# Recurrent mixer from norm to scan in one block: keys first, preparation tile by tile beside the projections

## The chip, the cores and the metric

One core of a Trainium2 chip. The metric is the device time of one execution in microseconds (us), the median of the runs. The engines are TensorE (PE in the profile, its weight loads PEld), VectorE (DVE), ScalarE (ACT), GpSimd (POOL) and SyncE (SP), which issues the weights' DMAs. Each has its own queue and runs it in order; they meet only at semaphores.

## What is computed

The whole kernel is a stack of four layers, each with a mixer and a feed-forward, on 512 tokens of width 1024. The change lies in the mixer of the second layer:

```
xx = token_shift(h) - h;  x_j = h + xx * mu[j]        # j: r, w, k, v, a, g
r, k, v = xr @ w_r, xk @ w_k, xv @ w_v
w = -softplus(-(w0 + tanh(xw @ w1) @ w2)) - 0.5
a = sigmoid(a0 + (xa @ a1) @ a2);  g = sigmoid(xg @ g1) @ g2
kk = k * k_k, each head (64 columns) divided by its length
k = k * (1 + (a - 1) * k_a);  decay = exp(-exp(w))
S_t = S_(t-1) diag(decay_t) - (S_(t-1) kk_t)(kk_t a_t)^T + v_t k_t^T;  y_t = S_t r_t
y = group_norm(y) * ln_w + ln_b + sum(r * k * r_k) * v
out = (y * g) @ w_o
```

The recurrence is computed in chunks of 128 tokens for 16 heads. A token's rates are summed within its chunk, and powers of the decay turn r, k, kk and kk*a into "hats", with which a chunk is matrix products and one triangular system. That system is solved by inverting diagonal blocks of 32 (a substitution of 31 steps) and three rounds of products.

## The kernel before

Activations lie transposed: 8 tiles of 128 features x 512 tokens (2 KB of a partition each) in `arena`, in groups of eight named XN, XX, MX, RR, KK, VV, WW, AA. A weight matrix streams through a ring of four slots in units of 128 x 1024. ScalarE copies each unit to a rounded type (`split_high`, L298, two buffers `high_r`), VectorE subtracts to get the rest (`split_low`, L303), and TensorE makes three products per block of 128 x 128 (`products`, L280 to L284), 24 per unit. The split of unit n+2 waits for unit n's products. `split_and_read` interleaves a unit's split with what ScalarE or VectorE do with finished tiles. The order of streams is `ORDER`; SyncE loads by it, always four units ahead.

`phase` opens a block: all engines meet at its end, and GpSimd clears its semaphores after it, one by one. The mixer (`rwkv`) is such blocks one after another:
- `rms_norm` (L472 to L484): sum of squares by TensorE, root on ScalarE, reciprocal and scaling on VectorE;
- the token shift (L771), and lora1 loaded;
- the low rank (L777 mixes on VectorE, L813 products): three inputs of 8 tiles in turn. GpSimd splits the mix for r (L786, L788);
- streams r, k, v. VectorE mixes ahead for the next one, GpSimd splits, ScalarE copies the results (L853);
- second low rank (L884) with sigmoids (L891), rates in WW and in-rates in AA;
- k * k_k, then `norm` per head (L443 to L484);
- k's factor, 32 scans (L922) that sum the rates, centring at token 64, subtraction, and GpSimd's r * k with ScalarE's r_k and TensorE's sums for the bonus (L943, L949, L956);
- three exponents of a whole group (L966 to L969) and four products of a whole group (L979 to L988);
- diagonal blocks: products (L1068), copies by ScalarE (L1089), v turned to tokens (L1076), transposes L1036 and L1039, and the substitution of the first half on VectorE (L1052, L1055);
- the scan: 16 units of four heads and one chunk; unit u is chunk u // 4, heads 4 * (u % 4) on, so a unit's state was last changed four units earlier. Masks L1305, states L1342 and L1344. The second half's substitution runs on GpSimd beside it;
- group norm (L1394 to L1406, square L1416, root L1418) with GpSimd's product of bonus and v (L1411), transposes, the gate.

## Time and profile before

| | |
|---|---|
| median of 3 runs | 3280.72 us (3279.76 to 3281.08) |
| the profiled execution: time, span | 3279.62 us, 3277.8 us |
| TensorE busy | 2874.6 us, 88% |
| VectorE, ScalarE, GpSimd busy | 1609.5, 997.7, 628.9 us |
| mean granted clock of TensorE | 0.928 |

A row of the timeline gives the start and length in us, the engine, the line and operation, what it writes and reads, how many were merged, and in brackets how long the engine stood idle before it and what ended that. A clock of 1.00 is 2.4 GHz, 0.50 is 1.2 GHz. An f32 product has two records, one of the rounded type has one.

### The profile page before, as it was taken

To read this page: it belongs to the slowest core of one execution; us is meant where nothing else is said; L and a number is where in the kernel's file an instruction comes from. 1 tells how busy PE (TensorE), PEld (TensorE's weight loads), DVE (VectorE), ACT (ScalarE), POOL (GpSimd) and SP (SyncE) were. 2 spreads that over 40 slices of the span, in tenths; PEclk is the share of its full clock that TensorE was granted. 3 is DMA by queue.
4 is the path that set the end of the run, shared out by engine and by line. 5 is a ranking of instruction groups with operands and counts; after the bars stand their busy time and mean duration, and the time that the engine had idled before them with its cause. 6 is when DMAs were issued, how large, how long until landed. Compare 5 with 4: busy or idle time off the path is not lost. (4 is left out here: it accounts for less than half of the span.)

```text
span 3277.8 us, 37985 instructions
## 1 busy us (share of the span) xinstructions
PE 2874.6 (88%) x13832; PEld 2279.5 (70%) x13832; DVE 1609.5 (49%) x2033; ACT 997.7 (30%) x1493; POOL 628.9 (19%) x573
## 2 busy tenths in 40 slices
PE   6799999698449959999979967579999987999999
PEld 4678888276248947888858856258888863688887
DVE  3377763621663457775342546555443335764432
ACT  3233332122231213333223243243222223732221
POOL 0031112320221003111100033253111101431110
PEclk9899999799678979999989977789999998999999
DMA  3123333122000002333313200113323320023333
GB/s 126 61 71 96 96 90 96 40 84 77 0 1 1 1 8 84 96 96 90 103 53 96 83 1 1 34 26 101 96 96 90 103 84 7 2 90 96 96 89 104
DMA packets 79432, 218.67 MB, mean 67 GB/s; under 512 B 21808, under 2 KB 21936, under 8 KB 78800
## 3 DMA queue, kind: packets, MB, share of 16 engines
q1 hardware_dynamic: 78880, 213.28, 21.5%
q10 hardware_dynamic: 432, 3.78, 0.3%
q8 instruction: 76, 1.25, 0.2%
q14 instruction: 44, 0.36, 0.0%
HBM read 214.93 MB, written 2.10 MB: 66 GB/s over the span
## 5 line engine op out<-in xcount | busy, mean ns | idle before, releaser
L280 PE MATMUL psum<-rounded,high_r 128*128 128x512 f32 x3104 | 1220.4, 393 | 61.1 <-DVE rounded L245 41.6
L282 PE MATMUL psum<-rounded,high_r 128*128 128x512 f32 x3104 | 1213.9, 391 | 0.0
L284 PE MATMUL psum<-rounded,ring_low 128*128 128x512 f32 x3104 | 1213.3, 391 | 0.0
L303 DVE TENSOR_TENSOR ring_low<-ring,high_r 128x1024 fp32r<-128x1024 f32 (+2 forms) x432 | 519.2, 1202 | 734.0 <-ACT high_r L298 732.7
L298 ACT ACTIVATE high_r<-ring 128x1024 fp32r<-128x1024 f32 (+2 forms) x432 | 421.2, 976 | 1490.8 <-PE psum L284 1466.8
L280 PEld LDWEIGHTS psum<-rounded,high_r 128*128 128x128 f32 x3104 | 586.4, 189 | 200.0 <-issue 51.2
L284 PEld LDWEIGHTS psum<-rounded,ring_low 128*128 128x128 f32 x3104 | 586.5, 189 | 122.8
L282 PEld LDWEIGHTS psum<-rounded,high_r 128*128 128x128 f32 x3104 | 587.0, 189 | 121.2 <-issue 1.0
L655 DVE TENSOR_TENSOR arena<-psum,inverse 128x512 f32<-128x512 f32 x176 | 121.5, 691 | 313.7 <-PE psum L284 313.5
L555 POOL CAST rounded<-rows 128x512 f32 (+1 forms) x88 | 53.8, 612 | 785.3 <-DVE rows L660 785.3
L1598 POOL TENSOR_SCALAR arena<-arena,small 128x512 f32<-128x512 f32 x64 | 99.6, 1563 | 196.8 <-DVE small L1567 195.8
L396 POOL TENSOR_TENSOR arena<-resid 128x512 f32<-128x512 f32 x49 | 63.9, 1303 | 335.5 <-DVE resid L384 335.5
L557 POOL TENSOR_TENSOR rounded<-rows,rounded 128x512 f32 (+1 forms) x88 | 115.8, 1316 | 13.2 <-POOL rounded L555 11.9
L455 PE MATMUL psum<-work,const 128*128 128x512 f32 x116 | 64.7, 721 | 54.0 <-ACT work L443 54.0
L401 POOL TENSOR_TENSOR square_sum<-square_sum,arena 128x512 f32<-128x512 f32 x49 | 90.8, 1853 | 3.8
L455 PEld LDWEIGHTS psum<-work,const 128*128 128x128 f32 x116 | 26.5, 236 | 90.8 <-ACT work L443 61.9
L384 DVE TENSOR_TENSOR resid<-psum,resid 128x512 f32<-128x512 f32 (+1 forms) x64 | 44.3, 692 | 88.2 <-PE psum L284 88.2
L516 PE MATMUL psum<-const,arena 128*128 128x128 f32 x216 | 34.2, 334 | 54.1 <-PEq L111 54.1
L1491 PEld LDWEIGHTS psum<-const,arena 128*128 128x128 f32 x384 | 43.5, 146 | 54.0 <-issue 50.3
L1993 POOL TENSOR_TENSOR arena<-arena,rows 128x256 f32<-128x256 f32 x32 | 21.5, 686 | 298.8 <-SPq L111 282.9
L624 ACT ACTIVATE work<-arena,vec 128x512 f32<-128x512 f32 x88 | 71.1, 808 | 12.5 <-DVE arena L655 12.5
L1479 PE MATMUL psum<-arena 64*128 64x512 f32 x192 | 61.4, 726 | 15.2 <-DVE arena L1546 11.3
(256 smaller groups left out, 2836.7 us busy)
## 6 DMA issues: line engine op xcount, KB each, us to landing
ring<-in_up SPq DMA_DIRECT2D x176, 512.0 KB, 3.5
ring<-in_down SPq DMA_DIRECT2D x64, 384.0 KB, 3.1
ring<-in_down SPq DMA_DIRECT2D x64, 320.0 KB, 2.9
ring<-in_even_in SPq DMA_DIRECT2D x36, 512.0 KB, 3.5
ring<-in_sgu_in SPq DMA_DIRECT2D x16, 512.0 KB, 3.5
ring<-in_even_out SPq DMA_DIRECT2D x16, 384.0 KB, 3.1
ring<-in_qkv SPq DMA_DIRECT2D x12, 512.0 KB, 3.4
ring<-in_sgu_out SPq DMA_DIRECT2D x8, 512.0 KB, 3.5
```

The lines of the kernel that those rows point to most:

```text
L280: nc.tensor.matmul(psum[:, m, :], high_r[:, r % HIGHS, blk], x_high, start=(k0 + k == 0), stop=False)
L282: nc.tensor.matmul(psum[:, m, :], high_r[:, r % HIGHS, blk], x_low, start=False, stop=False)
L284: mm = nc.tensor.matmul(psum[:, m, :], ring_low[:, r % R, blk], x_high, start=False, stop=end)
L298: nc.scalar.activation(high_r[:, r % HIGHS, 0:nk * P], ring[:, r % R, 0:nk * P], ACT.Copy).then_inc(unit_high, 1)
L303: nc.vector.tensor_tensor(ring_low[:, r % R, 0:nk * P], ring[:, r % R, 0:nk * P], high_r[:, r % HIGHS, 0:nk * P].bitcast(F32), ALU.subtrac ...
L396: nc.gpsimd.tensor_tensor(square, x, x, ALU.mult).then_inc(squared, 1)
L401: nc.gpsimd.tensor_tensor(square_sum[:, :], square_sum[:, :], square, ALU.add).then_inc(squares_summed, 1)
L455: nc.tensor.matmul(psum[:, 4, :], gather(i), square_sum[:, :] if squares_ready else work[:, i % 4, :], start=(i == 0), stop=(i == sums - 1 ...
L557: nc.gpsimd.tensor_tensor(tile_of(rounded(HL, KF), n), rows[:, 2 + pair, :], tile_of(rounded(HH, KF), n).bitcast(F32), ALU.subtract).then_ ...
L624: nc.scalar.activation(work[:, r, :], zs(r), ACT.Identity, bias=v1(g * R + (cb + r)), scale=v1(g * R + (cw + 88 + r))).then_inc(biased, 1)
L655: nc.vector.tensor_tensor(zs(r), psum[:, r, :], inverse[:, 0, :], ALU.mult).then_inc(scaled, 1)
L1598: nc.gpsimd.tensor_scalar(x, x, one(rc, i, e), None, ALU.mult).then_inc(sem, 1)
```

## The change

All from the norm to the end of the scan becomes one block with 65 semaphores, and nothing in it meets but by these.
- The order of streams is k, r, v. The norm, shift (now GpSimd's), mix and split for k go tile by tile.
- While k is multiplied, VectorE mixes per unit one tile of the three low-rank inputs and of r's and v's; TensorE runs that tile's low-rank products after the unit. ScalarE squares the finished keys, and TensorE sums them.
- In stream r, TensorE runs rates (now by token, so with the bias w0 as a 65th row) and in-rates after units 0 to 3. After units 4 to 7 it spreads the inverse lengths and sums the rates by products with a centred triangular matrix (`spread_and_sum`), which takes the scans' place. ScalarE takes exponents of a tile (`raise_powers`), VectorE forms its hats.
- v is computed by token (`token_products`: activations stationary, weights moving), so it needs no transposes. Units 2 to 5 carry tiles 4 to 7 of the preparation, units 0, 1, 6 and 7 the diagonal blocks. Both substitutions are on GpSimd, the first beside the stream v.
- The scan's units go by groups of tiles: 8 units for the first 8 heads, two per chunk, then 8 for the others, so a unit's state was last changed two units earlier.
- The bonus is formed after the scan, from the hats (the powers cancel): 8 products on GpSimd, scaled by ScalarE, summed by TensorE.

The diff at its core:

```diff
-        ORDER = ["sgu_in", "sgu_out", "up0", "down0", "rwkv_r", "rwkv_k", "rwkv_v", "rwkv_o", "up1", "down1",
...
+        ORDER = ["sgu_in", "sgu_out", "up0", "down0", "rwkv_k", "rwkv_r", "rwkv_v", "rwkv_o", "up1", "down1",
...
+                    if after_unit:
+                        after_unit(g * st.body + r)
...
+            carried = [heads(XN + 7), heads(XX + 7)]
+            solved = [heads(XX + b) for b in range(2)]
...
+                c, i0 = u % 8 // 2, 4 * (u // 8) + 2 * (u % 2)
...
+            def changes(u):
+                return u % 8 < 6
...
+                    def gather(i):
+                        pe.wait_ge(squared, i + 1)
+                        nc.tensor.matmul(psum[:, 7, :], head_sums(i), inverse[:, i % 2, :], start=(i == 0),
+                                         stop=(i == KD - 1)).then_inc(gathered, 1)
+
+                    def low_rank(n):
+                        if n == 0:
+                            pe.wait_ge(lw1_loaded, 16)
+                            pe.wait_ge(guarded, 1)
+                        pe.wait_ge(low_rank_mixed, 3 * n + 3)
+                        for at, m, to, x in ((0, 64, psum[0:HD, 4, :], 0), (64, 64, psum[HD:P, 4, :], 1),
+                                             (128, 128, psum[:, 5, :], 2), (256, 32, psum[0:32, 6, :], 2)):
+                            mm = nc.tensor.matmul(to, lw1[:, n, at:at + m], low_rank_in[x], start=(n == 0), stop=(n == KD - 1))
+                        mm.then_inc(low_rank_used, 1)
+                        if n:
+                            gather(n - 1)
...
+                    def spread_and_sum(i):
+
+                        if i == 0:
+                            pe.wait_ge(kk_inverted, 1)
+                            pe.wait_ge(rates_kept, 8)
+                            pe.wait_ge(a_kept, 8)
+                        if i == 4:
+                            pe.wait_ge(diagonal_kept, 4 * BLOCKS)
+                        if i:
+                            pe.wait_ge(powered, i)
+                        if i >= 2:
+                            pe.wait_ge(hats_done, i - 1)
+                        nc.tensor.matmul(psum[:, 4 + i % 2, :], head_spread(i), inverse[:, 0, :], start=True, stop=True).then_inc(spread_done, 1)
+                        for c in range(NCH):
+                            for k in range(2):
+                                mm = nc.tensor.matmul(psum[:, 6 + k, c * CH:(c + 1) * CH], rates[:, c, i * P:(i + 1) * P],
+                                                      con("centred", P, k * P), start=True, stop=True)
+                        mm.then_inc(summed, 1)
+
...
+                        if n % 4 == 0:
+                            pe.wait_ge(hats_done, n + 4)
...
+                    def with_r(n):
+                        if n == 0:
+                            gather(KD - 1)
+                        if n < 4:
+                            for m in (2 * n, 2 * n + 1):
+                                rate(m)
+                                in_rate(m)
+                        else:
+                            spread_and_sum(n - 4)
+
+                    def with_v(n):
+                        if n in (0, 1):
+                            pair_of_units(2 * n)
+                            pair_of_units(2 * n + 1)
+                        elif n in (6, 7):
+                            pair_of_units(2 * n - 8)
+                            pair_of_units(2 * n - 7)
+                        else:
+                            spread_and_sum(n + 2)
+
...
+                    products(pe, "rwkv_k", two_parts(RR, VV), k_taken, lambda k: pe.wait_ge(k_low, k + 1), after_unit=low_rank)
+                    products(pe, "rwkv_r", two_parts(MX, WW), r_taken, lambda k: pe.wait_ge(r_low, k + 1),
+                             lambda m: pe.wait_ge(k_taken, 5 + m), after_unit=with_r)
+                    token_products("rwkv_v", two_parts(VV, XN))
...
+                    def after_k(g, m, done):
+                        n = 4 * g + m
+                        done()
+                        nc.scalar.activation(tile(KK + n), psum[:, m, :], ACT.Copy).then_inc(k_taken, 1)
+                        act.wait_ge(k_taken, n + 1)
+                        if n >= 2:
+                            act.wait_ge(gathered, n - 1)
+                        else:
+                            act.wait_ge(normed, KD)
+                        nc.scalar.activation(inverse[:, n % 2, :], tile(KK + n), ACT.Square, scale=col("k_k", n)).then_inc(squared, 1)
+                        if n == KD - 1:
+                            act.wait_ge(low_rank_used, KD)
+                            act.wait_ge(v_mixed, KD)
...
+                    def raise_powers(i):
+                        act.wait_ge(summed, i + 1)
+                        if i:
+                            act.wait_ge(hats_done, i)
+                        grow, shrink_before = powers(i)
+                        before = psum[:, 7, :].rearrange("p (c t) -> p c t", c=NCH)[:, :, 0:1].rearrange("p c o -> p (c o)")
+                        nc.scalar.activation(shrink_before, psum[:, 7, :], ACT.Exp, scale=-EXP_HALF)
+                        nc.scalar.activation(grow, psum[:, 6, :], ACT.Exp, scale=EXP_HALF)
+                        nc.scalar.activation(chunk_in[:, i, :], before, ACT.Exp, scale=EXP_HALF)
+                        nc.scalar.activation(shrink[:, :], psum[:, 6, :], ACT.Exp, scale=-EXP_HALF).then_inc(powered, 1)
+
...
+                    def k_rest(i):
+                        dve.wait_ge(k_high, i + 1)
+                        nc.vector.tensor_tensor(rounded(VV)[:, i, :], tile(VV + i), rounded(RR)[:, i, :].bitcast(F32),
+                                                ALU.subtract).then_inc(k_low, 1)
+
+                    def k_mix(i):
+                        dve.wait_ge(shifted, 2 * i + 2)
+                        mix(2, i, tile(VV + i)).then_inc(k_mixed, 1)
+                    for i in range(KD):
+                        nc.vector.scalar_tensor_tensor(out=tile(XN + i), in0=resid[:, i, :], scalar=col("mix_g", 8 + i), in1=inverse[:, 0, :],
+                                                       op0=ALU.mult, op1=ALU.mult).then_inc(normed, 1)
+                        if i >= 2:
+                            k_mix(i - 2)
+                        if i >= 3:
+                            k_rest(i - 3)
...
+                    def during_k(g, m, done):
+                        n = 4 * g + m
+                        if n == 0:
+                            dve.wait_ge(lw1_loaded, 16)
+                        else:
+                            dve.wait_ge(low_rank_used, n)
+                        for which, to in zip((1, 4, 5), low_rank_in):
+                            mix(which, n, to).then_inc(low_rank_mixed, 1)
+                        mix(0, n, tile(WW + n)).then_inc(r_mixed, 1)
+                        mix(3, n, tile(XN + n)).then_inc(v_mixed, 1)
+
+                    def hats(i):
+
+                        grow, shrink_before = powers(i)
+                        kk, k, a, r = inverse[:, 1, :], tile(KK + i), tile(AA + i), tile(RR + i)
+                        dve.wait_ge(spread_done, i + 1)
+                        nc.vector.scalar_tensor_tensor(out=kk, in0=k, scalar=col("k_k", i), in1=psum[:, 4 + i % 2, :],
+                                                       op0=ALU.mult, op1=ALU.mult).then_inc(hat_steps, 1)
+                        dve.wait_ge(hat_steps, 6 * i + 1)
+                        dve.wait_ge(powered, i + 1)
+                        nc.vector.scalar_tensor_tensor(out=whole_w(i), in0=kk, scalar=-1.0, in1=shrink_before,
+                                                       op0=ALU.mult, op1=ALU.mult).then_inc(hat_steps, 1)
+                        dve.wait_ge(hat_steps, 6 * i + 2)
+                        nc.vector.scalar_tensor_tensor(out=shrink_before, in0=a, scalar=-1.0, in1=k,
+                                                       op0=ALU.add, op1=ALU.mult).then_inc(hat_steps, 1)
+                        dve.wait_ge(hat_steps, 6 * i + 3)
+                        nc.vector.scalar_tensor_tensor(out=k, in0=shrink_before, scalar=col("k_a", i), in1=k,
+                                                       op0=ALU.mult, op1=ALU.add).then_inc(hat_steps, 1)
+                        nc.vector.tensor_tensor(a, a, kk, ALU.mult).then_inc(hat_steps, 1)
+                        nc.vector.tensor_tensor(r, r, shrink[:, :], ALU.mult).then_inc(hat_steps, 1)
+                        dve.wait_ge(hat_steps, 6 * i + 5)
+                        nc.vector.tensor_tensor(k, k, grow, ALU.mult)
+                        nc.vector.tensor_tensor(a, a, grow, ALU.mult)
+                        ends = shrink[:, :].rearrange("p (c t) -> p c t", c=NCH)[:, 0:3, CH - 1:CH].rearrange("p c o -> p (c o)")
+                        nc.vector.tensor_tensor(scl[:, i, 0:3], ends, chunk_in[:, i, 1:4], ALU.mult).then_inc(hats_done, 1)
+
+                    def during_r(g, m, done):
+                        n = 4 * g + m
+                        if n == 0:
+                            dve.wait_ge(gathered, KD)
+                            nc.vector.tensor_scalar(inverse[:, 0, :], psum[:, 7, :], 1.0, 1e-24, ALU.mult, ALU.max).then_inc(kk_guarded, 1)
+                            dve.wait_ge(kk_rooted, 1)
+                            nc.vector.reciprocal(inverse[:, 0, :], inverse[:, 1, :]).then_inc(kk_inverted, 1)
+                        if n >= 4:
+                            dve.wait_ge(r_taken, n - 3)
+                            hats(n - 4)
+
+                    def during_v(g, m, done):
+                        n = 4 * g + m
+                        if n == 1:
+                            dve.wait_ge(diagonal_kept, 4 * BLOCKS)
+                            turn_in(0).then_inc(turned_in, 1)
+                        if 2 <= n < 6:
+                            dve.wait_ge(r_taken, n + 3)
+                            hats(n + 2)
+                    split_and_read(dve, "rwkv_k", split_low, during_k)
+                    split_and_read(dve, "rwkv_r", split_low, during_r)
+                    split_and_read(dve, "rwkv_v", split_low, during_v)
+                    dve.wait_ge(diagonal_kept, 8 * BLOCKS)
+                    turn_in(1).then_inc(turned_in, 1)
+                    dve.wait_ge(steps0, SUBSTITUTED)
+                    turn_back(0).then_inc(turned_back, 1)
...
+                    part(MX, WW, r_mixed, r_high, r_low)
+                    pool.wait_ge(unit_done, r_first)
+                    part(VV, XN, v_mixed, v_high, v_low)
+                    pool.wait_ge(unit_done, v_first)
+                    identity(pool, 0, steps0)
+                    pool.wait_ge(turned_in, 1)
+                    substitute(pool, 0, steps0)
+                    pool.wait_ge(unit_done, v_end)
                     nc.gpsimd.memset(state, 0.0).then_inc(cleared, 1)
+                    pool.wait_ge(summed, KD)
                     for x in solved:
                         nc.gpsimd.memset(x, 0.0).then_inc(cleared, 1)
-                    identity(pool, steps)
-                    substitute(pool, nc.gpsimd, steps)
+                    pool.wait_ge(hats_done, KD)
+                    identity(pool, 1, steps1)
+                    pool.wait_ge(turned_in, 2)
+                    substitute(pool, 1, steps1)
...
+                    dve.wait_ge(bonus_done, 1)
+                    nc.vector.tensor_copy(bonus, psum[:, 0, 0:64]).then_inc(bonus_kept, 1)
...
+                    for i in range(KD):
+                        nc.gpsimd.tensor_tensor(arena[:, KK + i, :], arena[:, RR + i, :], arena[:, KK + i, :], ALU.mult).then_inc(paired, 1)
+                    pool.wait_ge(bonus_kept, 1)
+                    nc.gpsimd.tensor_tensor(vw, vw, bonus.unsqueeze(2).to_broadcast([P, 64, HD]), ALU.mult).then_inc(done, 1)
...
+                    for i in range(KD):
+                        act.wait_ge(paired, i + 1)
+                        nc.scalar.activation(arena[:, KK + i, :], arena[:, KK + i, :], ACT.Copy, scale=col("r_k", i)).then_inc(rated, 1)
```

## Rows read from the trace of the kernel before

**Rows 1.** Stretches: length, busy PE, PEld, DVE, ACT, POOL, TensorE's clock, DMA share, GB/s

```profile
587.00:654.00 67.00, 40.30 (x66) 8.60 (x66) 46.09 (x44) 6.73 (x8) 22.67 (x18) 0.72 0.05 18
...
803.00:850.00 47.00, 33.70 (x64) 13.41 (x64) 12.83 (x19) 17.66 (x26) 0.00 (x0) 0.86 0.05 10
...
850.00:920.00 70.00, 14.08 (x66) 14.03 (x68) 57.87 (x59) 17.93 (x13) 21.27 (x9) 0.53 0.00 0
...
920.00:958.00 38.00, 14.71 (x160) 13.14 (x159) 26.90 (x65) 15.95 (x40) 1.11 (x2) 0.68 0.00 1
...
958.00:1171.00 213.00, 200.14 (x1776) 190.58 (x1776) 85.60 (x185) 42.68 (x108) 35.26 (x67) 0.92 0.01 1
```

**Rows 2.** Timeline of VectorE, norm ahead of the mixer (start, length, operation)

```profile
591.73 3.35 DVE L475 RECIPROCAL rows<-rows 128x512 f32<-128x512 f32 x1 [0.70 <-ACT rows L445]
...
595.12 5.39 DVE L484 SCALAR_TENSOR_TENSOR arena<-resid,vec,rows 128x512 f32<-128x512 f32 x8
```

**Rows 3.** Timeline of ScalarE and VectorE at the end of one projection unit

```profile
783.76 1.06 ACT L298 ACTIVATE high_r<-ring 128x1024 fp32r<-128x1024 f32 x1 [3.90 <-PE psum L284]
...
784.86 1.23 DVE L303 TENSOR_TENSOR ring_low<-ring,high_r 128x1024 fp32r<-128x1024 f32 x1 [4.21 <-ACT high_r L298]
```

**Rows 4.** Timeline of VectorE and GpSimd, mixing and splitting

```profile
606.49 32.16 DVE L777 SCALAR_TENSOR_TENSOR arena<-arena,vec 128x512 f32<-128x512 f32 x32 [1.16 <-DVE arena L772]
...
663.85 1.29 POOL L788 TENSOR_TENSOR rounded<-arena,rounded 128x512 fp32r<-128x512 f32 x1
```

**Rows 5.** Timeline: TensorE in the low rank, ScalarE at the second one

```profile
627.41 25.46 PE L813 MATMUL psum<-arena 128*64 128x512 f32 x48 [0.72 <-DVE arena L777]
...
811.12 0.69 ACT L891 ACTIVATE arena<-psum,vec 128x512 f32<-128x512 f32 x1 [0.17 <-PE psum L884]
```

**Rows 6.** TensorE's granted clock around a gap (third column), and the gap's end

```profile
751.00:752.00 1.00, 0.00 (x0) 0.60 0.69 274
...
757.00:758.00 1.00, 1.00 (x4) 0.50 0.00 0
...
758.00:759.00 1.00, 1.00 (x5) 0.99 0.00 0
...
754.60 0.77 PE L280 MATMUL psum<-rounded,high_r 128*128 128x512 f32 x1 [5.73 <-PEq L111]
```

**Rows 7.** Timeline of TensorE, f32 products of 128 columns

```profile
926.30 1.97 PE L1076 MATMUL psum<-const,arena 128*128 128x128 f32 x16
...
931.45 2.06 PE L1068 MATMUL psum<-arena 64*128 64x128 f32 x32
```

**Rows 8.** The substitution's additions on both engines (min/median/max, first and last start)

```profile
L1055 POOL TENSOR_TENSOR rows<-rows,square_sum x31: 252/584/732, 961.9 to 998.4; 128x31 f32<-128x31 f32 x2, 128x60 f32<-128x60 f32 x2, 128x87 f32<-128x87 f32 x2, 128x112 f32<-128x112 f32 x2
```

**Rows 9.** Timeline of ScalarE and VectorE, diagonal blocks to the scan's first mask

```profile
932.65 6.38 ACT L1089 ACTIVATE arena<-psum 32x256 f32<-32x256 f32 x16
...
954.13 1.91 DVE L1039 STREAM_TRANSPOSE arena<-rows 128x1024 f32<-128x1024 f32 x1
...
960.43 1.29 DVE L1305 TENSOR_TENSOR arena<-psum,const 128x512 f32<-128x512 f32 x2 [2.62 <-POOL arena L1373]
```

**Rows 10.** Timeline of VectorE in the scan: state kept, next values kept

```profile
1127.33 0.29 DVE L1344 TENSOR_TENSOR spare<-spare,small 64x128 f32<-64x128 f32 x1
...
1134.50 0.42 DVE L1312 COPY work<-psum 128x256 f32<-128x256 f32 x1 [1.66 <-PE psum L1164]
```

**Rows 11.** Timeline of VectorE, ScalarE and GpSimd after the scan

```profile
1171.30 4.42 DVE L1394 TENSOR_REDUCE small<-arena 128x64 f32<-128x4096 f32 x1 [5.31 <-PEq L111]
...
1172.77 7.05 POOL L1411 TENSOR_TENSOR arena<-arena,small 128x4096 f32<-128x4096 f32 x1 [174.08 <-issue]
...
1175.75 4.12 DVE L1396 TENSOR_SCALAR small<-small 128x64 f32<-128x64 f32 x1
...
1184.37 3.62 ACT L1416 ACTIVATE arena<-arena 128x4096 f32<-128x4096 f32 x1 [13.37 <-DVE arena L1398]
...
1193.58 4.43 DVE L1406 TENSOR_TENSOR arena<-arena,small 128x4096 f32<-128x4096 f32 x1
```

More of the change, by code:

```diff
@@ L1013, in rwkv, with squares_of_blocks @@
[L1013 removed]
+            carried = [heads(XN + 7), heads(XX + 7)]
+            solved = [heads(XX + b) for b in range(2)]
+            def squares_of_blocks(x):
+                return x.rearrange("p (a b) -> p a b", b=BLOCK)
+            diagonal = [squares_of_blocks(flat(rows[:, 0:2, :])), squares_of_blocks(span(XX + 2, 2))]
+            lower = [squares_of_blocks(span(WW, 2)), squares_of_blocks(span(XX + 4, 2))]
+            inv_flat = [span(WW + 2, 2), flat(inverse[:, :, :])]
```

566 lines of the change are left out of this document (248 added, 318 removed).

## Prediction

> **What bounds the kernel now.** I read four views, in this order. First the stretches of the recurrent mixer [rows 1]: from the end of the feed-forward before it (587) to the first mask of the scan (960) lie 373 us, in which TensorE's big products are only the three projections. One projection unit costs 1.23 + 4.21 = 5.44 us from one split to the next [rows 3], so 24 units are 131 us. The other 242 us belong to small stages run one after another: norm, shift and low rank (67), low-rank seconds and key norm (47), scans and exponents (70, TensorE busy 14 and at half clock), diagonal blocks and substitution on VectorE (38). Second, VectorE's timeline for the lengths of one operation [rows 2, 4]. Third, TensorE's granted clock around idle gaps [rows 6]. Fourth, the handoffs after the scan [rows 11]. Everything outside 587 to 1198 is not touched; the constants' load at the start grows a little, which I leave out of the sum as well under 1 us.
>
> **The change, placed in absolute time.** The cheapest way to sum so large a rewrite is to rebuild the new block's time line with the old durations and to see when its first mask would come, against 960.4 now [rows 9].
>
> *Start to first key unit.* The inverse root is ready at 595.1 as now [rows 2]. Then VectorE does 24 operations (scale, mix, remainder of each tile), 0.67 us each alone [rows 2], 16 us; GpSimd computes the shifts beside it. Where both ran on SBUF, 32 mixes took 32.16 us, 1.0 each, half as much again [rows 4]. Between 16 and 24 I take 21.5: last operand at 616.6, and the unit that waits for it ends at about 618. The two ends are 613 and 621.
>
> *Key stream.* After each of its 8 units TensorE's queue holds `low_rank(n)`, which waits for three mixes. VectorE issues these behind `split_low` of unit n+2, and that waits for ScalarE's split, which waits for unit n itself (buffers of two). So TensorE idles per unit: the handoffs and 1.06 + 1.23 us give 2.6 [rows 3], three mixes 2.0, together 4.6 us. Behind that wait stand the next unit and all of TensorE's queue. Then four f32 products of 512 columns and the sum of squares of the keys. Their price: 24 such products took 25.46 us, 1.06 each [rows 5], in a stretch whose clock was 0.72 in the mean [rows 1]; the second low rank's took 0.69 + 0.17 = 0.86 each [rows 5]. I take 1.0 at full clock: 5.0 us. The clock: a gap from 749 to 754.6 brought it to half, and it was full again only at 758, 3.4 us after work resumed [rows 6]; half speed for 3.4 us loses 1.7 us. Bounds for this loss are 0 and 1.7 per unit. I take 1.7, because the gap of 4.6 us is near the one in the rows and comes after every unit. A cycle is 5.44 + 4.6 + 5.0 + 1.7 = 16.7 us. The first has no squares to sum and ends its low rank at 628.3; seven more end at 745.2. The whole low rank so costs more than the 46 us it takes alone today (606.5 to 652.9 [rows 4, 5]); it is not hidden beside the projection, but put between its units.
>
> *Receptance stream.* Units 0 to 3 are followed by two rate and two in-rate products each, and one last square sum: 4 x 5.44 + 17 x 0.93 (between 0.86 and 1.0) = 37.6. ScalarE reads each unit's four while TensorE works on the next unit, so its table loads there are covered; uncovered they would cost TensorE the difference once, at unit 0. Now at 782.8. Units 4 to 7 are followed by a spread (0.95) and eight products of 128 columns, 16 records in 1.97 us or 0.25 each [rows 7]: 5.44 + 0.95 + 2.0 = 8.4 each, 33.6, now 816.4. The 32 scans of VectorE are gone, as are the whole-array exponents and products. VectorE's own loop here is powers on ScalarE (three exponents at 0.69, one tiny, handoffs: 2.5) and then seven SBUF operations, 5.2 us: 7.7, just under TensorE's 8.4, so it hides if nothing disturbs it.
>
> *Value stream to first mask.* Times from its start at 816.4. Unit 0 ends at 5.4; the diagonal products wait for the fourth tile (7.7) and cost 16 x 0.13 us [rows 7], 9.8; unit 1 and two more pairs, 17.3; ScalarE's 8 copies at 0.40 and VectorE's transpose of 1.9 [rows 9] let GpSimd start substitution 0 at 22. It takes 37.5 us there [rows 8], on top of four tiles of VectorE work. Undisturbed, VectorE finishes tile 7 at 58; with its operations lengthened by half [rows 4], 7.8 + 2.5 = 10.3 per tile, at 67. Two pairs, unit 7, two pairs: 68 to 77. Copies, two transposes of 1.9 and handoffs: 74 to 83. The substitution, 59.5 alone, is at 70 to 83 by the same disturbance, and the scan waits for it. I take 80 of 74 to 86: first mask at 896.4. That is 64.0 us earlier. What was removed, the VectorE substitution above all, is inside that number.
>
> The Trainium skill (SBUF — State Buffer, "SBUF: two separate sides") says that a GpSimd operation and a VectorE operation with two SBUF inputs lock each other out for the whole instruction. The mixes show only half of that, 1.0 in place of 0.67 us [rows 4], while the small operation at 1175.75 did stand until GpSimd's long one ended [rows 11]. By full exclusion each tile would take about 9 us plus 2.5, and the value stream would end near 86; by the mixes, near 80. The sum goes by the mixes.
>
> *Scan.* Same 16 units and same order on each engine; only the state is read two units later instead of four. The state was written by 1127.6 and the read of the next unit but one cannot come before the next unit's values at 1134.5 are past [rows 10], so there are over 5 us of slack. Zero, with 0 to +3.
>
> *After the scan.* Now: sum at 0 (1171.30), square on ScalarE at 13.1, last product at 22.3 to 26.7 [rows 11]. New: GpSimd's queue clears 65 semaphores in place of 21, which now delay it by 1.5 us [rows 11], so 4.5; then eight products of 1.29 to 1.6 us [rows 4], ending at 16.0. ScalarE's eight rate copies are queued ahead of its square, so the square waits for the last of them: 16.9 in place of 13.1. Second sum ends at 25.1, the bonus is kept at 25.4, and only then starts GpSimd's product of 7.05 us, which today runs in the shadow. VectorE's last product would meet it, as the small operation at 1175.75 met it and took 4.12 us, to GpSimd's very end [rows 11]: 32.6 + 4.4 = 37.0 in place of 26.7. Cost +10.3, between +4 (no meeting) and +13.
>
> **Sum.** -64.0 + 10.3 = -53.7 us. The profiled span of 3277.8 becomes 3224; that execution took 3279.6, 1.8 more than its span, and the median of the three runs is 3280.72, so 3280.72 - 53.7 = 3227.
>
> **Rivals.**
> *The loss of clock is small and the engines don't disturb each other.* For it: gaps of 4.6 us are shorter than the one in the rows, and the clock fell only some 3 us into it. Against: there it stood at half when work resumed. It gives -13.6 (8 x 1.7), -5 in the value stream, -4 after the scan and -4 at the start: down to 3200.
> *VectorE becomes the bound from the receptance stream on.* Its loop of 7.7 us is 0.7 below TensorE's, with GpSimd at work beside it for most of the time. If each of the seven operations takes a third more, both streams go by it (+6), substitution gates the scan (+6), the rest goes to its upper ends (+3 start, +3 scan, +3 tail) and waits in the key stream are 0.8 us longer (+6): 3254.
> *TensorE stays at half clock through the key stream; slower than before.* Place: each gap of 4.6 us. If the 3.4 us to recover never run out, each unit costs 5.44 more and its five small products 3.3 beyond the 1.7: 8.7 x 8 = +70, 3297. It decides from seven of eight units on (7 x 8.7 = 61 > 54). Against it: after 754.6 the clock recovered in 3.4 us of steady work [rows 6], and a cycle here has over 10 us of it.
> *The scan gives it back.* If each of the 12 changing units waited 2 us for its state, +24: 3251, still faster. [rows 10] speak against it.
> *The work isn't hidden.* Of the 242 us of small stages the sum saves only 64 less 10; that the change hides less than its shape suggests is already in the forecast.
>
> **How the numbers follow.** Forecast 3227: 0.55. Undisturbed 3200 to 3215: 0.18. VectorE bound 3240 to 3254: 0.15. Scan: 0.03. Half clock: 0.04. Something not seen that takes over 50 us: 0.05, of which half ends within 0.2% or slower. The range 3200 to 3254 holds the first four, some 0.85. A run can tell 0.2% (6.6 us) from no change: faster 0.92, same 0.02, slower 0.06.
>
> **What would show it.** Key units at a period of 16.7 us with TensorE idle 4.6 in each and a granted clock near 0.8; receptance units 4 to 7 at 8.4; first mask at about 896; the square of the group norm behind the rate copies, and VectorE's last product of that norm ending 37 us after its first sum. Wrong would be: key units below 14 us, first mask after 915 or before 880, or a scan longer than 213 us.

## The result, and the profile after

The kernel after takes 3236.06 us (median of 4 runs, 3235.97 to 3237.95) against 3280.24 us for the kernel before on the same chip (4 runs, 3279.03 to 3281.08): a ratio of 0.9867, with a 95% interval of 0.985 to 0.9884. It is faster by 44 us, or 1.3%; the interval leaves out no change. The forecast was 3227, within 3200 to 3254. The profiled spans are 3277.8 and 3236.1 us, a difference of 41.7.

The stretches of the changed block are the first view of the kernel after, with the columns of [rows 1]:

```profile
587.00:618.00 31.00, 12.89 (x25) 6.97 (x26) 26.20 (x26) 6.95 (x10) 17.02 (x18) 0.51 0.16 55
618.00:748.00 130.00, 94.28 (x250) 43.31 (x249) 36.31 (x48) 20.74 (x27) 22.63 (x21) 0.79 0.10 33
748.00:820.00 72.00, 72.00 (x299) 49.78 (x298) 30.39 (x38) 33.32 (x52) 12.76 (x14) 1.00 0.19 59
820.00:900.00 80.00, 66.90 (x424) 55.26 (x423) 50.72 (x54) 31.11 (x66) 49.37 (x71) 0.94 0.17 53
900.00:1117.00 217.00, 201.66 (x1744) 192.13 (x1744) 86.11 (x187) 42.48 (x108) 31.19 (x59) 0.89 0.01 1
1117.00:1156.00 39.00, 14.11 (x65) 13.97 (x66) 25.34 (x8) 10.82 (x11) 21.08 (x9) 0.50 0.05 17
```

They are the start, the streams of k, r and v, the scan and what follows it. Only the stream r (748 to 820) fills TensorE at full clock. The stream k leaves 36 us of 130 idle and runs at 0.79. The first mask of the scan comes at 900.30 instead of 960.43 [rows 9], so the block gains 60.1 us up to there. Behind it two stages are longer than before. These are VectorE's rows in the kernel after that answer to [rows 9] and [rows 11]:

```profile
900.30 2.44 DVE L1370 TENSOR_TENSOR arena<-psum,const 128x512 f32<-128x512 f32 x4
...
1116.67 4.42 DVE L1493 TENSOR_REDUCE small<-arena 128x64 f32<-128x4096 f32 x1 [5.31 <-PEq L112]
...
1145.15 10.40 DVE L1507 TENSOR_TENSOR arena<-arena,small 128x4096 f32<-128x4096 f32 x1
```

From the first mask to the first sum the scan takes 216.4 us; before, 960.43 to 1171.30, it took 210.9: +5.5. From that sum to the end of the last product it takes 38.9 us; before it took 26.7: +12.2. The account is -60.1 + 5.5 + 12.2 = -42.4 us, against the 41.7 of the spans; the other 0.7 lies outside these stretches.

### The profile page after: what moved, and what is told of

It reads as the page before. It is cut to its first block and busy times, and to the rows that moved or that the text cites. A ratio compares the mean times of both kernels' runs of the same rounds, so it can differ in the third digit from the quotient of the medians.

```text
span 3236.1 us, 38094 instructions
## 1 busy us (share of the span) xinstructions
PE 2901.8 (90%) x13928; PEld 2294.1 (71%) x13928; DVE 1573.0 (49%) x1974; ACT 1000.3 (31%) x1522; POOL 666.3 (21%) x634
## 5 line engine op out<-in xcount | busy, mean ns | idle before, releaser
L281 PE MATMUL psum<-rounded,high_r 128*128 128x512 f32 x3040 | 1200.2, 395 | 65.3 <-DVE rounded L246 41.0
L283 PE MATMUL psum<-rounded,high_r 128*128 128x512 f32 x3040 | 1189.8, 391 | 0.0
L285 PE MATMUL psum<-rounded,ring_low 128*128 128x512 f32 x3040 | 1189.3, 391 | 0.0
L281 PEld LDWEIGHTS psum<-rounded,high_r 128*128 128x128 f32 x3040 | 574.6, 189 | 210.2 <-issue 56.7
L283 PEld LDWEIGHTS psum<-rounded,high_r 128*128 128x128 f32 x3040 | 575.5, 189 | 119.6 <-issue 2.6
L285 PEld LDWEIGHTS psum<-rounded,ring_low 128*128 128x128 f32 x3040 | 574.9, 189 | 120.5
L560 POOL TENSOR_TENSOR rounded<-rows,rounded 128x512 f32 (+1 forms) x88 | 116.4, 1323 | 13.1 <-POOL rounded L558 11.9
L458 PE MATMUL psum<-work,const 128*128 128x512 f32 x100 | 56.6, 730 | 48.8 <-ACT work L446 48.8
L904 PE MATMUL psum<-arena 128*64 128x512 f32 (+2 forms) x64 | 46.1, 1085 | 35.7 <-DVE arena L856 35.7
L1586 PE MATMUL psum<-arena 64*128 64x512 f32 x192 | 61.5, 727 | 15.1 <-DVE arena L1653 11.2
```

The lines of the kernel that those rows point to most:

```text
L281: nc.tensor.matmul(psum[:, m, :], high_r[:, r % HIGHS, blk], x_high, start=(k0 + k == 0), stop=False)
L283: nc.tensor.matmul(psum[:, m, :], high_r[:, r % HIGHS, blk], x_low, start=False, stop=False)
L285: mm = nc.tensor.matmul(psum[:, m, :], ring_low[:, r % R, blk], x_high, start=False, stop=end)
L458: nc.tensor.matmul(psum[:, 4, :], gather(i), square_sum[:, :] if squares_ready else work[:, i % 4, :], start=(i == 0), stop=(i == sums - 1 ...
L560: nc.gpsimd.tensor_tensor(tile_of(rounded(HL, KF), n), rows[:, 2 + pair, :], tile_of(rounded(HH, KF), n).bitcast(F32), ALU.subtract).then_ ...
```

## The experiments

All edits are to the kernel after, unless said otherwise. Single runs have no interval. They are read by their profiles, and the change in their time only serves as a check.

**The wait in the stream k.** The first two experiments ask what a unit's period consists of. In the kernel after, one period looks like this on VectorE (splits and mixes) and TensorE (low-rank products):

```profile
635.10 1.22 DVE L306 TENSOR_TENSOR ring_low<-ring,high_r 128x1024 fp32r<-128x1024 f32 x1 [10.96 <-ACT high_r L301]
636.24 3.39 DVE L856 SCALAR_TENSOR_TENSOR arena<-arena,vec 128x512 f32<-128x512 f32 x5
...
652.16 1.23 DVE L306 TENSOR_TENSOR ring_low<-ring,high_r 128x1024 fp32r<-128x1024 f32 x1 [12.52 <-ACT high_r L301]
...
638.36 5.83 PE L904 MATMUL psum<-arena 128*64 128x512 f32 x8 [4.45 <-DVE arena L856]
644.12 1.36 PE L894 MATMUL psum<-inverse,const 128*128 128x512 f32 x2
```

The split at 635.10 had itself waited 10.96 us for ScalarE, the mixes stand behind it, and TensorE stands for them. The period is 652.16 - 635.10 = 17.06 us. The first experiment only puts VectorE's mixes ahead of its split:

```diff
-                    split_and_read(dve, "rwkv_k", split_low, during_k)
+                    split_and_read(dve, "rwkv_k", split_low, early=during_k)
```

> One edit to the changed kernel: VectorE issues the mixes of tile n ahead of the split of unit n+2 (from the second tile on), so they run while unit n is multiplied. Theory A (the changed kernel's key stream is long because TensorE waits for mixes queued behind a split, and because its clock falls in that wait): the 4.45 us of idle and the half clock both go; the period of a key unit falls from 17.06 to 5.44 + 4 x 1.05 + 0.9 = about 10.5 us, the granted clock in the stretch from 0.79 to 1.00, and seven such periods save 46 us: 3190 us. Rival B (the small products between the units, or VectorE, set the period, and the wait only takes a place that something else would take): the period stays above 14 us and the kernel above 3215 us.

Measured: 3189.26 us (3186.12 to 3191.64), ratio to the kernel before 0.9727 (0.971 to 0.9743). The first mask is at 848.03, 52.3 us earlier; scan and tail stay (215.9 and 38.9). These are VectorE and TensorE in two of its periods, and TensorE's weight loads in the second:

```profile
644.12 1.22 DVE L306 TENSOR_TENSOR ring_low<-ring,high_r 128x1024 fp32r<-128x1024 f32 x1 [4.28 <-ACT high_r L301]
646.01 3.40 DVE L856 SCALAR_TENSOR_TENSOR arena<-arena,vec 128x512 f32<-128x512 f32 x5 [0.67 <-PE psum L904]
653.70 1.22 DVE L306 TENSOR_TENSOR ring_low<-ring,high_r 128x1024 fp32r<-128x1024 f32 x1 [4.29 <-ACT high_r L301]
...
652.44 3.11 PE L904 MATMUL psum<-arena 128*64 128x512 f32 x8
655.48 1.13 PE L894 MATMUL psum<-inverse,const 128*128 128x512 f32 x2
...
652.44 0.20 PEld L904 LDWEIGHTS psum<-arena 128*64 128x64 f32 x4 [0.35 <-issue]
653.45 0.30 PEld L904 LDWEIGHTS psum<-arena 128*128 128x128 f32 x2 [0.81 <-issue]
654.51 0.14 PEld L904 LDWEIGHTS psum<-arena 128*32 128x32 f32 x2 [0.76 <-issue]
655.48 0.30 PEld L894 LDWEIGHTS psum<-inverse,const 128*128 128x128 f32 x2 [0.84 <-ACT inverse L1156]
```

The period is 653.70 - 644.12 = 9.58 us: 5.44 for the unit and 4.14 for the small products. That is theory A, with a period still shorter than its 10.5. From 629 to 701 TensorE is busy 72.00 of 72.00 us, at a clock of 1.00. The idle 4.45 us were the order of VectorE's queue and nothing else, since nothing else was changed. 7 periods x (17.06 - 9.58) = 52.4, which is the 52.3 at the mask. The medians differ by less, 3236.06 - 3189.26 = 46.8: the profiled execution, 3186.12, is the fastest of its four, two others took 3191, and why those are slower no profile shows. The rows also correct a price. Five f32 products of 512 columns take 4.1 us, not 5.0, because both 64-column products, which write different halves of the PSUM partitions, start within the one slot of 1.01 us between the loads at 652.44 and 653.45. The Trainium skill (TensorEngine Tiling (Array Packing), "Key Properties") says that separate tiles of the array can load and multiply in parallel; this trace agrees for two tiles of 64 columns.

The second experiment keeps the wait and fills it, so that only the clock changes:

```diff
+                        if n >= 3:
+                            pe.wait_ge(k_taken, n - 2)
+                        for _ in range(20):
+                            nc.tensor.matmul(psum[:, (n + 1) % 4, :], rounded(RR)[:, 0, 0:P], rounded(RR)[:, 0, :], start=True, stop=True)
                         pe.wait_ge(low_rank_mixed, 3 * n + 3)
```

The products stand ahead of that wait and nothing reads them; from n = 3 on they wait for `k_taken` n - 2, so that their bank is free.

> Order of the changed kernel kept; while TensorE waits for the mixes after each key unit it makes 20 products of the rounded type that nobody reads (20 x 0.227 = 4.5 us, as long as the wait). This leaves the wait and takes only the fall of the clock away. Theory A (the forecast took 1.7 us per unit for the clock): the period falls from 17.06 to about 15.4 us, the kernel by 12 to 13 us to about 3223 us. Rival B (the clock costs nothing there, the small products are just longer than 1 us): the period stays at 17.0 to 17.3 us and the kernel at 3236 to 3238 us.

Measured: 3214.73 us (one run), 21.3 below the kernel after; the stretches of e2 and of the kernel after:

```profile
618.00:724.00 106.00, 106.00 (x406) 68.30 (x405) 36.30 (x48) 19.70 (x26) 19.16 (x17) 1.00 0.12 40
```

```profile
638.00:644.00 6.00, 5.64 (x8) 0.98 (x8) 1.63 (x3) 0.00 (x0) 2.33 (x2) 0.50 0.00 0
644.00:646.00 2.00, 2.00 (x6) 1.26 (x6) 0.00 (x0) 0.00 (x0) 0.00 (x0) 0.84 0.00 0
646.00:651.00 5.00, 4.97 (x22) 3.75 (x20) 0.00 (x0) 0.00 (x0) 0.00 (x0) 1.00 0.00 0
```

With the wait filled, the period is 14.11 us (= 5.44 + 4.5 + 4.1) and the clock stays full. So the clock cost 17.06 - 14.11 = 2.95 us per unit. 7 x 2.95 = 20.7 is most of the 23.2 us by which the first mask comes earlier (877.15); the first period, 13.54 in place of 15.50, and the start give the rest. The second fence shows why it is not 1.7: after each wait the clock is at half from 638.4 to nearly 645, about 6.5 us, and [rows 6] had shown 3.4. The expectation of -12 to -13 missed this.

**The scan.** Between these kernels VectorE's copies of a unit's values (`z`, once a unit) serve as a ruler. At full clock most of their 15 intervals are 12.1 to 12.6 us; the first is 9.74, and a few lie between 10.8 and 13.8 at fixed places. Three are off in the kernel after: the first takes 15.09 us (9.74 before), and the sixth and seventh take 14.83 and 20.71. The kernel before has 13.73 and 20.56 at the seventh and eighth, and 14.95 at the third. The two copies that bound the first interval, then TensorE and its stretches at the start and in the middle of the scan, kernel after:

```profile
905.64 0.42 DVE L1377 COPY arena<-psum 128x256 f32<-128x256 f32 x1 [2.91 <-PE psum L1053]
920.73 0.42 DVE L1377 COPY arena<-psum 128x256 f32<-128x256 f32 x1 [1.26 <-PE psum L1053]
...
901.96 2.05 PE L1038 MATMUL psum<-arena 128*128 128x128 f32 x8 [5.83 <-ACT arena L1233]
...
982.37 0.59 PE L1051 MATMUL psum<-spare,work 128*128 128x128 f32 x2 [1.71 <-issue]
...
906.00:916.00 10.00, 9.88 (x58) 9.19 (x59) 2.17 (x6) 0.00 (x0) 8.90 (x15) 0.50 0.01 2
...
982.00:994.00 12.00, 11.63 (x60) 11.44 (x62) 2.21 (x7) 0.38 (x1) 0.00 (x0) 0.52 0.00 1
```

Ahead of the first carry TensorE stands 5.83 us, because the first substitution's result has to be turned by VectorE and spread by ScalarE while nothing else is left to multiply. That result was there long before, at 890.9. Its turn stands in VectorE's queue behind that of the second half's blocks, which waits for their last copies (14.18 us idle):

```profile
896.70 1.90 DVE L831 STREAM_TRANSPOSE arena<-arena 128x1024 f32<-128x1024 f32 x1 [14.18 <-ACT arena L1198]
898.52 1.90 DVE L834 STREAM_TRANSPOSE rows<-arena 128x1024 f32<-128x1024 f32 x1
```

No run exchanged the two. After the pause the clock is at half until 917. The fourth kernel fills that pause with products that nothing reads:

```diff
                     pe.wait_ge(diagonal_kept, 8 * BLOCKS)
+                    for _ in range(26):
+                        nc.tensor.matmul(psum[:, 7, :], rounded(VV)[:, 0, 0:P], rounded(VV)[:, 0, :], start=True, stop=True)
                     carry(0)
```

> Ahead of the scan's first carry, where TensorE stands idle 5.8 us for the first inverse, it makes 26 products that nobody reads. Theory A (the scan is 5.5 us longer than before because this pause leaves TensorE at half clock for the first 15 us): the clock stays at 1.00, the first unit takes about 10 to 12 us instead of 15.1, the kernel is 3 to 6 us shorter: 3230 to 3233 us. Rival B (the units by groups of tiles are longer by themselves): the scan stays at 216 us and the kernel at 3236 us.

Measured: 3223.26 us (one run), 12.8 below the kernel after, more than either theory gave. The mask is at 899.64 (900.30 in the kernel after), and the scan takes 203.6 us instead of 216.4. The scan of e4, to be read against the stretch from 900 to 1117 of the kernel after (clock 0.89):

```profile
899.00:1103.00 204.00, 191.22 (x1757) 181.61 (x1756) 86.06 (x186) 42.48 (x108) 31.41 (x59) 0.96 0.01 1
```

The first unit is at 9.74 again, 5.35 us less, and the stretch from the mask to the first copy falls from 5.34 to 4.05. Later profiles bear this out: the first interval is 9.73 and 9.74 in the two later kernels with the same filling, and 15.04 to 16.14 in the six changed kernels without it. So the half clock behind the pause costs 6.6 us, more than the whole +5.5. The scan of the kernel before was no scan at full clock either: by the intervals beside them its 14.95 holds 2.8 us of half clock and its 20.56 another 8.4. An estimate without them is 210.9 - 11.2 = 199.7 us, and the last kernel below, at full clock until 19 us before its end, takes 200.2. So the new order of units costs next to nothing, as forecast. The rest of the gain was not expected: the pair 14.83 and 20.71 has become 13.73 and 12.20 (9.6 us), and one later unit takes 15.32. Filling the start also moved or removed a half-clock stretch 80 us later; one run does not show which.

**The first substitution.** The fifth kernel cuts GpSimd's first substitution to one step of 31:

```diff
-                for n, t in enumerate(range(BLOCK - 1, 0, -1)):
+                for n, t in enumerate(range(BLOCK - 1, 0, -1) if b else [1]):
...
-                    dve.wait_ge(steps0, SUBSTITUTED)
+                    dve.wait_ge(steps0, 4)
```

> The first substitution, on GpSimd beside the value stream, is cut to one of its 31 steps (its result is then wrong; all other work is kept). Theory A (beside GpSimd's small operations VectorE's operations on SBUF take 1.0 to 1.2 us instead of 0.69, and with them its tile is the bound of the value stream): the last three tiles' period falls from 9.9 to about 8.1 us, the first mask comes some 6 to 8 us earlier (900.3 to 893), the kernel is 5 to 8 us shorter: 3228 to 3231 us. Rival B (TensorE's own work sets the end of the stream): the operations are shorter but the mask comes at 899 to 900 and the kernel stays at 3234 to 3236 us.

Measured: 3232.32 us (one run), 3.7 below the kernel after (its profiled span 5.6 below), where 5 to 8 were expected. VectorE's rows for one tile in the stream v, first the kernel after, then e5:

```profile
855.16 0.99 DVE L1318 SCALAR_TENSOR_TENSOR arena<-inverse,arena 128x512 f32<-128x512 f32 x1
856.19 0.99 DVE L1321 SCALAR_TENSOR_TENSOR arena<-arena 128x512 f32<-128x512 f32 x1
...
859.18 1.19 DVE L1327 TENSOR_TENSOR arena<-arena,shrink 128x512 f32<-128x512 f32 x1
```

```profile
860.78 0.69 DVE L1318 SCALAR_TENSOR_TENSOR arena<-inverse,arena 128x512 f32<-128x512 f32 x1 [1.36 <-ACT shrink L1191]
861.50 0.69 DVE L1321 SCALAR_TENSOR_TENSOR arena<-arena 128x512 f32<-128x512 f32 x1
...
864.11 0.68 DVE L1329 TENSOR_TENSOR arena<-arena 128x512 f32<-128x512 f32 x1
```

The substitution does lengthen VectorE's operations from 0.68 to between 1.0 and 1.2 us, and GpSimd pays as well: its substitution lasts from 840.8 to 890.9, 50.1 us against 37.5 alone [rows 8]. Without it the last tiles' period falls from some 9.9 us to 8.12, and the mask comes 11.0 us earlier, at 889.30, where 6 to 8 were expected. TensorE's row behind the last tile, first in the kernel after, then in e5, shows of what:

```profile
882.58 3.79 PE L960 MATMUL psum<-arena 64*128 64x128 f32 x32 [8.17 <-DVE small L1332]
```

```profile
873.64 2.06 PE L960 MATMUL psum<-arena 64*128 64x128 f32 x32 [1.06 <-DVE small L1332]
```

VectorE's last tile is ready 8.9 us sooner, and the half clock behind TensorE's wait of 8.17 us, 1.7 us on this row, goes with it. The end of the substitution itself did not hold up the mask: it is at 890.9, and VectorE turned the result only at 898.52. The pause ahead of the first carry is 5.82 us here too, though 30 of 31 steps are gone. But the scan then takes 222.2 us (+5.8), at a clock of 0.87, its first units 16.14 and 18.49 us. Half of what the earlier mask gave is lost to the clock. The mechanism of the stream v is confirmed: in its last tiles VectorE is the bound. The time does not follow from it alone.

**After the scan.** Two kernels take the tail apart. The third moves GpSimd's eight products r * k into the second half of the scan (tiles 4 to 7 into `work`, which is free by then):

```diff
+                    pool.wait_ge(steps1, SUBSTITUTED)
+                    pool.wait_ge(y_done, 8)
+                    for i in range(KD):
+                        nc.gpsimd.tensor_tensor(pair_at(i), tile(RR + i), tile(KK + i), ALU.mult).then_inc(paired_early, 1)
...
-                    for i in range(KD):
-                        nc.gpsimd.tensor_tensor(arena[:, KK + i, :], arena[:, RR + i, :], arena[:, KK + i, :], ALU.mult).then_inc(paired, 1)
```

> GpSimd's eight products of r and k for the bonus are moved from after the scan into its second half, where GpSimd has nothing to do. Theory A (after the scan ScalarE's square waits behind eight rate copies that wait for these products, and GpSimd's product of 7.05 us then meets VectorE's last one): the square starts 13 us after the first sum instead of 19, the bonus is kept early, the long product falls under VectorE's sums, and the stretch from the first sum to the end of the last product falls from 38.9 us to 27 to 29 us: 3225 us. Rival B (GpSimd beside the scan delays the state updates): the scan is 3 us or more longer and the kernel above 3229 us.

The seventh is the third without the long product of bonus and v:

```diff
-                    nc.gpsimd.tensor_tensor(vw, vw, bonus.unsqueeze(2).to_broadcast([P, 64, HD]), ALU.mult).then_inc(done, 1)
```

> As the kernel with the bonus products in the scan, and GpSimd's long product of v and bonus (7.05 us) left out, so the output lacks the bonus's weight. Theory A (VectorE's last product of the group norm takes 10.4 us because it stands until that product ends): it takes 4.4 us, the stretch from the first sum to its end 22.8 instead of 28.75 us, the kernel 6 us less than 3227.4: 3221 us. Rival B (the last product is slow by itself or by its operands): it stays at 10.4 us and the kernel at 3227 us.

Measured: 3227.38 us (3226.77 to 3228.38, ratio to the kernel before 0.9841, 0.9825 to 0.9857) and 3221.45 us (one run). The scan is unchanged (216.3), and the tail falls from 38.9 to 28.75 and to 22.8 us. GpSimd and ScalarE in the kernel after:

```profile
1121.26 14.03 POOL L1513 TENSOR_TENSOR arena<-arena 128x512 f32<-128x512 f32 x8 [185.53 <-SPq L112]
1144.22 7.05 POOL L1515 TENSOR_TENSOR arena<-arena,small 128x4096 f32<-128x4096 f32 x1 [8.92 <-DVE small L1501]
...
1135.96 3.60 ACT L1523 ACTIVATE arena<-arena 128x4096 f32<-128x4096 f32 x1
```

Its last product on VectorE in e3, with GpSimd's long one beside it, and then in e7:

```profile
1134.26 7.05 POOL L1520 TENSOR_TENSOR arena<-arena,small 128x4096 f32<-128x4096 f32 x1 [105.30 <-DVE small L1508]
...
1135.19 10.40 DVE L1514 TENSOR_TENSOR arena<-arena,small 128x4096 f32<-128x4096 f32 x1
```

```profile
1136.02 4.43 DVE L1514 TENSOR_TENSOR arena<-arena,small 128x4096 f32<-128x4096 f32 x1
```

In the kernel after, ScalarE's square comes 19.3 us after the first sum (13.1 before, [rows 11]), behind the eight products, and VectorE's last product stands until GpSimd's has ended at 1151.27. The first costs 6.2 us, the second 6.0 (10.40 against 4.43 alone): 12.2, the whole loss. Moving the eight products did more than end the first: the square now comes 9.1 us after the first sum, earlier than the 13.1 before, because GpSimd's long product no longer holds up the small operation between first sum and subtraction (4.12 us at 1175.75, [rows 11]). VectorE's subtraction, which had met the eight products, is also shorter (5.45 to 4.42). That is the gain of 10.1. It did not end the meeting with the long product, since the bonus is kept only behind VectorE's second sum. So the tail of 28.75 lies in the expected 27 to 29 by two errors that cancelled: the square 4 us earlier than expected, and the meeting, which was to go, still there. The seventh kernel shows the price of that meeting: without the long product the operation takes 4.43 us, as its theory A said.

**The three edits together**, e1, e3 and e4 in one kernel, and then that kernel with one more pause filled:

> The mixes ahead of the split, the bonus products in the scan and the filled start of the scan in one kernel. Alone they saved 46.8, 8.7 and 12.8 us against 3236.1. Theory A (they are three separate places on the path): the savings add up, 3236.1 - 68.3 = 3168 us. Rival B (the scan's clock depends on more than its start, so that its saving of 12.8 us is partly chance of this placement): 3172 to 3180 us.

Measured: 3170.17 us (3160.3 to 3171.64), ratio 0.966 (0.9642 to 0.9677). Mask at 849.25, tail 28.75. The time lies between the two forecasts. The scan takes 209.6 us and not e4's 203.6, as the rival had it, because the pair in the middle is there again, 14.66 and 20.86. The half clock begins where VectorE turns the second inverse and TensorE stands 1.70 us. The last kernel puts two f32 products, which nothing reads, into that stop:

```diff
+                        if u == 6:
+                            pe.wait_ge(y_kept, 5)
+                            for _ in range(2):
+                                nc.tensor.matmul(psum[:, 7, :], con("ident"), arena[:, VV, :], start=True, stop=True)
                         corrections_in(u)
```

> The kernel is e6_all_three with one thing added: ahead of unit 6's corrections, where TensorE stands 1.70 us while VectorE turns the second inverse (924.61 [1.70] in e6), it has two f32 products of 512 columns that nothing reads, about 1.0 us each. Theory A (the short stop itself sets off the half clock that lasts from about 926 to 945 in e6): the intervals between the z copies there, 14.66 and 20.86, become about 12.9 and 12.2, and the time falls by 9 to 10 us from 3170: 3160 to 3162; if the half clock then comes later in the scan, less. Rival B (the half clock comes at a place of its own, whatever this stop does): both intervals stay near 14.7 and 20.9, and the time is 3170 to 3171. Rival C (the products only delay the unit behind them): 3171 to 3172, with the interval of 14.66 longer by up to 0.5.

Measured: 3159.81 us (3158.69 to 3165.37), ratio 0.9639 (0.9623 to 0.9655), and the scan takes 200.2 us. The stretch of the stop, first in e6, then in e8:

```profile
924.00:930.00 6.00, 5.39 (x27) 5.42 (x28) 0.93 (x3) 0.03 (x1) 0.00 (x0) 0.58 0.00 0
930.00:936.00 6.00, 6.00 (x33) 5.78 (x34) 1.44 (x5) 0.38 (x1) 0.00 (x0) 0.50 0.00 0
936.00:942.00 6.00, 6.00 (x39) 5.43 (x37) 1.76 (x4) 0.00 (x0) 0.00 (x0) 0.50 0.00 0
942.00:948.00 6.00, 5.44 (x34) 5.33 (x34) 2.08 (x5) 1.83 (x5) 0.00 (x0) 0.71 0.01 3
```

```profile
924.00:930.00 6.00, 6.00 (x49) 5.29 (x48) 1.49 (x4) 0.53 (x2) 0.00 (x0) 1.00 0.00 0
930.00:936.00 6.00, 6.00 (x67) 5.57 (x65) 4.14 (x10) 0.42 (x1) 0.00 (x0) 1.00 0.00 0
```

Theory A held in the profiled executions: with the stop filled, the clock stays full, and the intervals are 13.74 and 12.20 instead of 14.66 and 20.86, 9.6 us less. The first is above the 12.9 expected, since the products fill the stop but do not shorten it. The first copies lie 0.1 us apart and the five intervals ahead of the stop agree within 0.01 us, so the two executions differ little up to there but in the filling. The stop alone does not explain the half clock, though. One of e6's four executions took 3160.3 us with the stop unfilled, one of e8's took 3165.37 with it filled, and e4 has the same stop at full clock. This version beats the kernel before by 3.6% and the kernel after by 76 us.

## Why the prediction was right, and where its steps were off

The sign and the size came out, and the mechanism in every stage but the scan, but the forecast of -53.7 was 11.3 us too good against the profiled -42.4. The steps:

- **Start.** Forecast root 595.1, end of the first key unit 618; measured 594.6 and 618. Right.
- **Stream k.** Forecast period 16.7 us, measured 17.06, so right, but by errors that cancelled. The idle wait was 4.45 (4.6 forecast). The small products were 4.1 (5.0 forecast, since the overlap of the 64-column pair was not seen). The clock took 2.95 (1.7 forecast, from the recovery after one gap; and in that gap the clock fell 2.3 us after TensorE had stopped, where the prediction read 3). It ended at about 748 in place of 745.
- **Stream r.** Periods of 9.69 and 8.12 us (9.2 and 8.4 forecast); the f32 products of 64 and 65 rows took 1.05 each, above the 0.86 to 1.0 allowed. It ended 3.5 us later than forecast, most of it brought along from the stream k. VectorE did not bind: TensorE was busy 72.00 of 72.00.
- **Stream v.** Forecast 80, measured 80.4, again by errors that cancelled: VectorE's tile took 9.7 to 10.1 us (10.3 forecast) and the last was done after 62.5 (67 forecast), but the pairs and the unit behind it took 11.8 (10 forecast), 1.7 of it half clock. The forecast had the scan wait for the substitution, which ended after 71 and held up nothing. Full exclusion had put the end near 86. The Trainium skill (SBUF — State Buffer, "SBUF: two separate sides") has a GpSimd operation and a VectorE operation with two SBUF inputs lock each other out for a whole instruction. The trace shows two things: against the small operations of the substitution VectorE's took 1.0 to 1.2 in place of 0.68, half to three quarters as long again, and against the product of 7.05 us VectorE's stood to the very end (10.40 against 4.43). The second is the rule as it stands. With small ones both engines' operations are longer; that they wait for each other in short turns is argued, not shown. The forecast by the mixes was the nearer one.
- **Scan.** Forecast 0 with 0 to +3, measured +5.5, and its 216.4 us are past the 213 that the prediction had named as a sign of being wrong. This step failed. It asked only whether a state would be late, and that was not the trouble: at full clock the new order costs next to nothing. It did not ask what TensorE does while the first substitution's result is turned and spread, now that VectorE does this behind the last copies of the second half: it stands 5.83 us, and e4 shows that the half clock behind that pause is the 5.35 us of the first unit and 1.3 ahead of it.
- **After the scan.** Forecast +10.3, measured +12.2. Both parts were there, the square behind the rate copies (6.2 against 3.8 forecast) and the meeting with GpSimd's long product (6.0). The term that was too small is that of the eight products: 14.03 us, 1.75 each, in place of 1.29 to 1.6.

The error of 11.3 is then 3.9 up to the mask, 5.5 in the scan and 1.9 behind it. Of the rivals, VectorE as the bound came only in the stream v, where the forecast already had it (TensorE waits 8.17 us for its last tile), and not from the stream r on. The half clock that never recovers did not either, for the clock was full again within each period. The scan gave something back, as one rival said, but by the clock and not by the state. The chances of the first four outcomes add up to 0.91, not to the 0.85 given to the range.

## What to carry to other kernels

When work is interleaved, look at the order inside each engine's queue: one line that put a unit's mixes ahead of a split was worth more (47 us) than the whole change had gained (44). The same question stands open at the scan's start, where a finished result waits in VectorE's queue behind a turn that is not ready. For every pause of TensorE that an edit leaves or makes, price the half-clock time behind it apart from the pause; filling the pause with products that nothing reads measures that price (2.95 us per unit in e2, 6.6 in e4), and may be worth keeping. After the start of a stage is moved, look again at pauses far behind it.

## What the runs showed of the hardware that was not expected

In the scan, half-clock stretches several times as long as the stop ahead of them come and go. In the scan of the kernel before, TensorE stood 1.70 us ahead of 1049.82; its stretches there are:

```profile
1050.00:1052.00 2.00, 2.00 (x18) 2.00 (x18) 0.42 (x1) 0.80 (x3) 0.00 (x0) 0.89 0.00 0
1052.00:1066.00 14.00, 14.00 (x79) 13.21 (x78) 3.19 (x8) 0.39 (x1) 0.00 (x0) 0.50 0.01 1
```

The clock is at half while TensorE is busy for 14.00 of 14.00 us, and is back only about 18 us after the stop, where a wait of 4.45 us in the stream k was followed by 6.5 us of half clock and the gap in [rows 6] by 3.4. The same stop of 1.70 us left the clock at 1.00 in e4 (ahead of 975.06), and did not in e6 (ahead of 924.61). Nor does it take such a stop. In the kernel before the clock also fell at 986.7 and stayed at half until about 993.5, the 2.8 us in the interval of 14.95, and the longest stop shown in the 9 us ahead of it is 0.61 us (ahead of 984.71). TensorE alone (length, busy, clock, DMA share, GB/s):

```profile
985.00:987.00 2.00, 2.00 (x19) 0.93 0.03 8
987.00:989.00 2.00, 2.00 (x11) 0.50 0.00 0
```

In e4 it fell the same way at 1012.3, 2.5 us behind a stop of 0.61 us; that is the interval of 15.32. So the length of a pause does not give its price, and what filling one gains holds for the place and the kernel where it was measured. What sets the price was not settled; neither was why one of e6's four executions, which has no profile, took 3160.3 us.
